# Front of a fused two-block kernel: six buffer slots for the first ten weight chunks, the root ahead of the weight copies, four sums in one PSUM bank, and constant products on TensorE

## The reference, cut to what matters

```python
def rms_norm(x, g, eps=RMS_EPS):
    x32 = x.astype(jnp.float32)
    y = x32 * lax.rsqrt(jnp.mean(x32 * x32, axis=-1, keepdims=True) + eps)
    return (y * g.astype(jnp.float32)).astype(x.dtype)
...
        mod = (jax.nn.silu(c) @ w_ada[l] + b_ada[l])[:, None, :]
        sh1, sc1, gt1, sh2, sc2, gt2 = jnp.split(mod, 6, axis=-1)
        xn = rms_norm(h, norm1_g[l]) * (1.0 + sc1) + sh1
        proj = xn @ w_in[l]
        qm, km, vm, zrw, gate_logits = jnp.split(proj, split_at, axis=-1)
```

## Time and profile before

| what | us |
|---|---|
| three runs: lowest, median, highest | 1714.99, 1715.53, 1727.62 |
| the profiled execution, its own time | 1728.51 |
| its span | 1726.7 |
| mean granted TensorE clock | 0.969 |

### The profile page before, as it was taken

One profiled execution on the slowest core, in us unless ns is written; L12 is line 12 of the kernel. 1 busy time (PEld: TensorE's weight loads), 2 busy tenths in 40 slices (PEclk: granted clock), 3 DMA queues, 4 the chain that ended last, 5 costly groups with the idle time before them and its releaser, 6 DMA issues.

```text
span 1726.7 us, 27227 instructions
## 1 busy us (share of the span) xinstructions
PE 1648.2 (95%) x11462; PEld 1496.7 (87%) x11462; DVE 1135.5 (66%) x1971; ACT 818.2 (47%) x1184; POOL 123.2 (7%) x54
## 2 busy tenths in 40 slices
PE   5889999988999999999999999999999998999998
PEld 4679987888999999998899888888898787999996
DVE  4495655665699789996544576666674464556675
ACT  3545533434444444444444444544434655455663
POOL 0000330100548100000000000000000000000000
PEclk8899996999999999999999999999999998999999
DMA  8543330344454554545655586666655344445331
GB/s 331 216 162 104 117 147 26 124 170 138 158 194 171 196 177 160 178 172 170 206 216 188 194 294 255 219 220 219 251 191 174 125 158 145 167 147 177 126 129 64
DMA packets 48604, 301.08 MB, mean 174 GB/s; under 512 B 5601, under 2 KB 6113, under 8 KB 15970
## 3 DMA queue, kind: packets, MB, share of 16 engines
q1 hardware_dynamic: 43586, 290.81, 47.6%
q10 hardware_dynamic: 4896, 8.54, 1.3%
HBM read 288.71 MB, written 9.44 MB: 173 GB/s over the span
## 4 chain that ended last, share of the span: by engine, by line
PE 86%; DVE 8%; ACT 4%; DMA 1%; issue 1%; SPq 0%; DVEq 0%; ACTq 0%
PE ps L605 85%; DVE WL L2011 2%; DVE ar L1984 2%; ACT ar L1398 1%; DVE ar L1995 1%; ACT WH L1406 1%; DVE ar L2320 1%; DMA vec<-in_vec 0%; ACT L1398 0%; PE ps L798 0%; DVE ar L2003 0%; DMA ar<-in_in_wag 0%; DVE ar L2145 0%; ACT X L1883 0%; PE ps L1315 0%
## 5 line engine op out<-in xcount | busy, mean ns | idle before, releaser
L2011 DVE TENSOR_TENSOR WL<-ar,WH 128x1024 fp32r<-128x1024 f32 (+1 forms) x428 | 503.4, 1205 | 343.5 <-ACT WH L1406 341.5
L605 PE MATMUL ps<-RH,WH 128*128 128x256 f32 x2136 | 630.3, 295 | 20.9 <-DVE WL L2011 5.6
L605 PE MATMUL ps<-RL,WH 128*128 128x256 f32 x2136 | 611.8, 286 | 0.0
L605 PE MATMUL ps<-RH,WL 128*128 128x256 f32 x2136 | 611.3, 286 | 0.0
L1406 ACT ACTIVATE WH<-ar 128x1024 fp32r<-128x1024 f32 (+1 forms) x478 | 481.8, 1042 | 255.8 <-PE ps L605 244.1
L605 PEld LDWEIGHTS ps<-RH,WH 128*128 128x128 f32 x2136 | 417.5, 195 | 29.0 <-DVE WL L2011 7.7
L605 PEld LDWEIGHTS ps<-RL,WH 128*128 128x128 f32 x2136 | 417.9, 196 | 0.9 <-issue 0.2
L605 PEld LDWEIGHTS ps<-RH,WL 128*128 128x128 f32 x2136 | 417.2, 195 | 0.0
L605 PE MATMUL ps<-WH,RH 128*128 128x512 f32 (+1 forms) x832 | 325.2, 391 | 5.4 <-DVE RL L2514 4.3
L605 PE MATMUL ps<-WH,RL 128*128 128x512 f32 (+1 forms) x832 | 321.6, 387 | 0.0
L605 PE MATMUL ps<-WL,RH 128*128 128x512 f32 (+1 forms) x832 | 321.5, 386 | 0.0
(11 more groups left out here) (155 smaller groups left out, 947.6 us busy)
## 6 DMA issues: line engine op xcount, KB each, us to landing
ar<-in_u SPq DMA_DIRECT2D x64, 1024.0 KB, 5.0
ar<-in_v SPq DMA_DIRECT2D x64, 1024.0 KB, 4.9
ar<-in_adr SPq DMA_DIRECT2D x16, 1024.0 KB, 5.5
ar<-in_ada SPq DMA_DIRECT2D x8, 1024.0 KB, 9.3
ar<-in_in_g SPq DMA_DIRECT2D x8, 1024.0 KB, 5.0
ar<-in_wq SPq DMA_DIRECT2D x8, 1024.0 KB, 4.8
far_gates<-ar ACTq DMA_DIRECT2D x32, 256.0 KB, 2.0
ar<-far_gates SPq DMA_DIRECT2D x16, 512.0 KB, 3.9
```

The costliest lines, as they stand in the source:

```text
L605: ins = q.matmul(o, l, r, start=start and i == 0, stop=stop and i == len(pairs) - 1, skip_group_check=skip)
L2011: q.tensor_tensor(l[:, x:z, :], src[:, x:z, :], h[:, x:z, :].bitcast(F32), ALU.subtract).then_inc(*v.up(("lo", n, i)))
```

## The change

- `FIRST_SLOTS` gives the first ten chunks the slots 0, 1, 2, 3, 4, 5, 0, 1, 2, 4. They no longer move the counter `n`, which now begins at 0 with the eleventh chunk, and `adr` begins its turn of the extra slots at the first of them.
- ScalarE's root of the norm stands ahead of the two `hi` copies of `in_wag`; the order of `ada_rows`, `first` and the `hi` copies of `in_rkv` changes.
- The sums 0 to 3 go side by side into bank 5, which leaves the ring with five banks; VectorE reads them when sum 3 is there.
- TensorE multiplies constants by constants (128 x 128 x 128, never read) at three places: 8 times at the start, 10 times behind sum 4, 4 times ahead of `by_tile(rkv, 0)`. Each group writes the ring's next bank and waits until its last content was read.
- The row tiles of the two projections stand in another order among `ada` 5 to 7.

```diff
@@ -64,6 +64,7 @@
 ZDOTS = (0,) * 8 + (4, 0, 2, 0, 2, 0, 2) + (0,) * 13
 DOTS = ((0, 0, 0, 2, 0, 0, 0, 2, 0, 2, 0, 2), (0, 2, 0, 0) * 3, (0,) * 16)
 EARLY = 12
+FIRST_SLOTS = (0, 1, 2, 3, 4, 5, 0, 1, 2, 4)
 LATE_LOADS = {36: 12, 44: 13, 52: 14, 58: 15}
 LATE_DOTS = {(2, 7): 12, (2, 15): 13, (3, 4): 14, (3, 11): 15}
 UNITS = ((2,) * 12, (1,) * 8 + (2,) * 4, (1, 0) * 5 + (1, 2, 2, 1, 1, 0))
@@ -132,9 +133,11 @@
     slots, n, e = [], 0, 0
     mixed = range(CHUNKS.index(("in_v", 0)), CHUNKS.index(("adr", EARLY - 1)) + 1)
     for c, (name, j) in enumerate(CHUNKS):
-        if c >= LATER:
+        if c < len(FIRST_SLOTS):
+            slots.append(FIRST_SLOTS[c])
+        elif c >= LATER:
             slots.append((c - LATER) % MANY)
-        elif name == "ada" and 3 <= j < 6 or name == "adr" and j < 5:
+        elif name == "adr" and j < 5:
             slots.append(FEW + e % 3)
             e += 1
         elif c in mixed:
@@ -605,6 +608,14 @@
             ins = q.matmul(o, l, r, start=start and i == 0, stop=stop and i == len(pairs) - 1, skip_group_check=skip)
         return ins
 
+    def constants(n):
+
+        b = ring["ids"][ring["at"] % len(ring["ids"])]
+        if b in holder:
+            p.wait_ge(*on(("out", holder[b])))
+        for _ in range(n):
+            mm(m.ps[b][:, 0:P], [(ones, ones)])
+
     def mm3(o, trip, start=True, stop=True, skip=False):
         pairs = []
         for lh, ll, rh, rl in trip:
@@ -777,7 +788,12 @@
     def ada_sum(j):
 
         p.wait_ge(*on(("out", ("ada", j))))
-        b = bank(("ada sum", j))
+        if j == 0:
+            give(5, ("ada sum", 3))
+        if j < 4:
+            b = m.ps[5][:, 2 * j:2 * j + 2]
+        else:
+            b = bank(("ada sum", j))
         for f in range(2):
             ins = mm(b[:, f:f + 1], [(m.ada_rows[j % 2][:, f * P:(f + 1) * P], cst("sel"))])
         ins.then_inc(*p.up(("ada sum", j)))
@@ -1022,7 +1038,8 @@
 
     def front():
         p.wait_ge(m.con_load, 16)
-        ring["ids"] = list(range(6))
+        ring["ids"] = list(range(5))
+        constants(8)
         ada(0)
         ada(1)
         ada_sum(0)
@@ -1038,27 +1055,25 @@
         key = ("in_rkv", 2 * KRV[0])
         rkv = take(), give(6, key), key
         ada_sum(4)
-        for k in range(3):
+        constants(10)
+        by_tile(wag, 0)
+        by_tile(wag, 1)
+        ada(5)
+        ada_sum(5)
+        by_tile(wag, 2)
+        by_tile(wag, 3)
+        ada(6)
+        ada_sum(6)
+        constants(4)
+        for k in range(4):
+            by_tile(rkv, k)
+        by_tile(wag, 4)
+        ada(7)
+        ada_sum(7)
+        by_tile(rkv, 4)
+        for k in range(5, 8):
             by_tile(wag, k)
-        ada(5)
-        by_tile(wag, 3)
-        ada_sum(5)
-        by_tile(wag, 4)
-        by_tile(rkv, 0)
-        by_tile(rkv, 1)
-        ada(6)
-        by_tile(wag, 5)
-        by_tile(rkv, 2)
-        by_tile(rkv, 3)
-        ada_sum(6)
-        by_tile(rkv, 4)
-        ada(7)
-        by_tile(wag, 6)
-        by_tile(rkv, 5)
-        ada_sum(7)
-        by_tile(rkv, 6)
-        by_tile(wag, 7)
-        by_tile(rkv, 7)
+            by_tile(rkv, k)
         ring["ids"], ring["at"] = list(range(7)), 0
         dots = dot_chunks()
         zs = with_dots(chain(iter([None] * 8), proj_steps("in_rkv", 0, js=KRV[1:])), dots)
@@ -1507,10 +1522,10 @@
         AC(m.XN, m.X, ACT.Square, "x squared")
         for j in range(3):
             ada_rows(j)
+        a.wait_ge(*on(("norm1", "rec")))
+        AC(m.rs, m.rs, ACT.Sqrt, "rs")
         for _ in range(2):
             feed.take()
-        a.wait_ge(*on(("norm1", "rec")))
-        AC(m.rs, m.rs, ACT.Sqrt, "rs")
 
         def first(k):
             a.wait_ge(*on(("modulation", k)))
@@ -1518,20 +1533,19 @@
                          bias=m.mod[:, k:k + 1]).then_inc(*a.up(("xs", "hi", k)))
 
         ada_rows(3)
+        ada_rows(4)
         first(0)
-        ada_rows(4)
-        first(1)
-        first(2)
         for _ in range(3):
             feed.take()
+        first(1)
+        ada_rows(5)
+        first(2)
         first(3)
-        ada_rows(5)
+        ada_rows(6)
         first(4)
-        first(5)
-        ada_rows(6)
-        first(6)
         ada_rows(7)
-        first(7)
+        for k in range(5, 8):
+            first(k)
         for _ in range(5):
             feed.take()
 
@@ -2118,8 +2132,8 @@
 
         for k in range(8):
             t = ("ada sum", k)
-            b = tile(t)
-            v.wait_ge(*on(t))
+            b = m.ps[5][:, 2 * k:2 * k + 2] if k < 4 else tile(t)
+            v.wait_ge(*on(("ada sum", max(k, 3))))
             q.scalar_tensor_tensor(mod[:, 48 + k:49 + k], b[:, 0:1], mod[:, 56 + k:57 + k], vc("n1", k),
                                    ALU.add, ALU.mult).then_inc(*v.up())
             q.tensor_tensor(mod[:, k:k + 1], b[:, 1:2], vc("b_ada", k), ALU.add).then_inc(*v.up(("modulation", k)))
```

## The result

| | runs | lowest | median | highest | profiled run, span |
|---|---|---|---|---|---|
| before | 4 | 1714.99 | 1718.56 | 1727.62 | 1728.51, 1726.7 |
| after | 4 | 1742.89 | 1744.43 | 1746.44 | 1744.68, 1742.8 |

The ratio of the times is 1.0143, with a 95% interval of 1.0099 to 1.0187: slower, and by more than the forecast of 1730.4 and its range up to 1739. Two gaps have to be told apart: the profiled executions differ by 16.1 us of span, which is near the 14.9 us of the forecast's sum; the medians differ by 26.

The account below looks back on a forecast made before the run. TensorE, with 86% of the chain, was taken to bound the kernel. Front 4, `in_v` 0 2.7, `in_g` 3 6.2 and clock 2 summed to 14.9 us, on the median 1715.53 giving 1730.4; range 1716 to 1739.

Parts of the forecast that it names:

- The sum: Whole kernel: 4 + 2.7 + 6.2 + 2 = 14.9 us, put on the median 1715.53 to give 1730.4, 0.9% slower.
- Front, +4: Start of the kernel to the last product of the front: ends 4 us later, bounds -1.6 and +6.5.
- The path to the first modulation: Early front: root at 18.4 to 18.8, scaling to 21.1, `lo` to 23.45, which is 1.85 us earlier.
- the stop: Front, after `wag` 2: TensorE stands from 35.1 to 37.9, until modulation 4 and the following steps are done.
- The next 3 or so us of work double: Front, behind the stop at 35.1: if the clock is lowered again, the front ends +5.8 instead of +2.8.
- `in_v` 0, +2.7: Load of `in_v` 0 now waits for the last `in_rkv` chunk; its `lo` ends 2.7 us later, bounds 1.5 to 3.7.
- `in_g` 3, +6.2: Load of `in_g` 3 waits for `adr` 11, its copies delay TensorE's step 10: 6.2 us, bounds 5.2 and 7.2.
- Clock behind it, +2: After TensorE's 6 us standstill for `in_g` 3 the clock falls: 2 us lost, bounds 0 and 3.5.
- The constants do hold the clock: Rival on the front: constant products keep the clock high, front -1.6, total 9.3, 1725; chance 0.2.
- Everything at its upper end: Rival: front +6.5, `in_v` +3.7, `in_g` +7.2, clock +3.5, together 20.9, 1736; chance 0.2.
- The low-rank stage: Rival "Not slower": the clock survives the stop at 50 to 54 us, this stage gains 7.7, total -0.4, 1715; chance 0.05.
- Nothing hid `in_g` 3: Rival: the wait for `in_g` 3 is hidden by other TensorE work or an earlier dot product, 6.7, 1722; chance 0.1.

Follow-up runs that it names:

- one for each slot: Two versions of the changed kernel: slot counter started at 9, so in_v 0 follows an earlier chunk, 1734.57; one slot number skipped at in_g 3, 1735.94.
- the filled one: Changed kernel plus four constant products in the recurrence's second step, ahead of the wait for the state: 1736.33.
- the run with the late loads alone: Kernel before, its front, order and constants untouched, with in_v 0 behind the last in_rkv chunk and in_g 3 behind adr 11: 1737.10, ratio 1.0123.
- both slots put back: Changed kernel with counter started at 9 and one slot number skipped at in_g 3, so both loads follow early chunks again: 1723.43, ratio 1.003.

## Why the prediction was right and wrong

**The sum was near for the execution it was made from, and wrong for the medians.** The step that failed is "it lies 13 us over the median of the three runs, which the measurement goes by: 1715.53 + 14.9": it carries the terms from the profiled run to the median as if what lifts that run lay elsewhere. What lifts it is TensorE's low clock, for the most part in two places: the long stretch just behind the second wait (27 us at 0.50, 6.8 us of time) and the three brief ones (some 4 us). The change makes both the rule. On the same kind of execution it costs 16 us; against the usual one another 10 come to it, which is 1728.5 + 16 and not 1715.5 + 15. Of 100 runs of the kernel before, on four chips, 59 took under 1718.1, 22 up to 1723 and 19 from 1728 to 1735 (none of these on the fourth chip, with 13 runs); the profiled ones were of the last group. The changed kernel shows the long stretch and all three brief ones in its profile, and its four runs lie within 3.6 us. That 14.9 came so near to 16.1 has some luck in it: the front was 2.4 too low and the clock 0.9, and 2.1 were won back on the way that no term had.

**Front, +4: mis-sized, +6.4** in this profile, 0.1 under its upper bound. The path to the first modulation came out as worked out (18.28 and 23.21, for 18.4 to 18.8 and 23.45), so did the ten constants (29.4 for 29.8), the wait of `first(2)` behind `ada_rows(5)` and the stop (34.5 to 36.8, for 35.1 to 37.9). What was mis-sized is the low clock behind the stop. "The next 3 or so us of work double" gave +3; the clock was low from 36.8 to 46.3, and the work from the stop to the end took 19.0 us instead of 14.3. 2.8 - 1.1 (the stop ended sooner) + 4.7 = 6.4. This term varies from run to run: in the three other profiles of the same front (one for each slot, and the filled one) it ended at 53.8 to 53.9, +4.4 to +4.5, near the +4. By parts: order +5.1, constants +2.3 to +4.2 (1.4 by the profile without the ten and the four), root and bank -3.2 to -4.1, six slots nothing. The forecast gave the freed sum 3 no gain of its own; the bank was worth 2.8 on the old front. That VectorE waits for sum 3 cost nothing, as said.

**`in_v` 0, +2.7: right** (2.7), load of 4.89 us included. **`in_g` 3, +6.2: right** (6.0), and TensorE stood for 5.42 us. The Trainium skill's sum for a load ("DMA: Bandwidth & Descriptors", anatomy of one DMA: 2.0 us and the bytes at 436 GB/s, for transfers issued from GpSimd), which is an estimate of 4.4 us, was 0.4 to 0.5 under the 4.89 and 4.76 us of these two.

**Clock behind it, +2: the term that was mis-sized.** The first low stretch cost 2.9, within its bounds of 0 to 3.5. The second, from 274 on, I had not asked about, though the profile of before showed it, nor about the three brief ones. The 20.3 us of the run with the late loads alone come apart as 9.7 up to the wait (8.7 for the stops and 2.9 behind the second, less 1.9 won back), 6.9 for the long stretch and 3.7 behind it.

**The rivals.** "The constants do hold the clock" was half right: the ten bring it back and it is lost again 7 us later, and they stand in the path themselves. The Trainium skill's rule that activity releases the throttle ("TensorE: Matmul & The Clock Gate", part 1) agrees with the trace behind the ten (0.50 until 29.4, then 1.00) and, by the durations, behind the eight (`ada` 0 and 1 in 2.99 us for 3.39). It doesn't explain the long stretch, where TensorE is listed busy for 26.47 of 27 us and the clock stays at 0.51. "Everything at its upper end" (1736) has the right sign and is still 8 short. The low-rank stage stayed low in every trace (14.6 to 15.5 us). Nothing hid `in_g` 3.

**Open.** What brings the long stretch isn't settled. By the profiles, it is there with both loads late (the changed kernel, the one without constants, the old front), with `in_v` 0 late alone, and in both profiles of the kernel before; it isn't with `in_g` 3 late alone (two traces). By the times, which tell less: both late, 12 of 12 in three kernels; `in_v` 0 alone, 6 of 10; `in_g` 3 alone, 1 of 8 on the new front and perhaps 2 of 3 on the old; neither, 1 of 10 with both slots put back, but 19 of 100 in the kernel before itself. So the two together make it the rule, and `in_v` 0 has the larger say; for `in_g` 3 alone nothing is shown. The wait of 1.03 to 1.04 us ahead of the piece can't be the whole cause, for it stands in every trace in which it wasn't filled, with the long stretch or without. Why the delay of `in_v` 0, 150 us earlier, has so much say isn't settled either; a shift of everything before it by 4 us had none. And why the three brief stretches mostly go with the long one, no run tells: two versions have the three without it.

## What to carry to other kernels

Where single runs fall into groups, ask to which of them the profiled run belongs before a sum is put on a median, and list the stretches of low clock in it, to its end and not only near the change: each is a cost that the change can make permanent or remove. A change of buffer slots at the start renames every later slot of a running counter; here that cost 20 of 26 us, and a few lines in the counter took it back. Filler products on TensorE belong only where it would stand still anyway: in a wait of 1.0 us they won 8 us of the median in the kernel that had the long stretch in every run, and nothing in one that seldom had it; in the path ten of them cost 4.2 us by themselves.

## What the runs showed of the hardware

- The same thin piece of the recurrence takes 24.1 to 24.2 us (eight traces), 25.7 to 26.1 (four) or 31.0 to 31.1 (six), by how much of it the clock is low. The wait ahead of it is 1.03 to 1.04 us in all but the two filled ones.
- The same stop can cost the clock or not: TensorE stands still for 2.41 us ahead of 788 us in the kernel before, and the clock is 0.50 behind it; with both slots put back it stands still for 2.41 us at the same place, and the clock stays at 1.00. Three such places make some 4 us.
- At the start TensorE can run at the low speed with a granted clock of 1.00 in the profile's rows: 16 products in 1.93 us instead of 1.07. There the durations tell the clock, not the column; it was so in five of the eighteen traces; none of them lists the low stretch at 20 to 34 us, and yet the three of them with the old front ended it at 51.0 to 51.2, for 49.4 and 49.7 in the kernel before.
